# Moving the split of the unit of weights three ahead in front of the step of the side work

## The chip, the cores and the metric

The kernel runs on one core of a Trainium2 chip. The metric is the device time of one execution, in microseconds (us). TensorE (PE in the profile) multiplies matrices, ScalarE (ACT), VectorE (DVE) and GpSimd (POOL) do the elementwise work, and SyncE (SP) issues nearly all transfers from HBM.

## The reference

Two transformer blocks follow each other on one sequence of 256 tokens with 1024 features, all in fp32. What is computed, cut to the calls:

```python
# first block
proj = rmsnorm(x, norm_mix_pre) @ w_in            # split into ten parts
ya = gla_mixer(...) @ w_branch_a                  # chunked gated linear attention
yb = pool_mixer(...) @ w_branch_b                 # trailing means
yc = moba_mixer(...) @ w_branch_c                 # softmax attention with a bias
mixed = gs0 * ya + gs1 * yb + gs2 * yc            # sigmoid gates
x = x + rmsnorm(mixed @ w_out, norm_mix_post)
h = rmsnorm(x, norm_ffn_pre)
x = x + rmsnorm((silu(h @ w_gate) * (h @ w_up)) @ w_down, norm_ffn_post)
# second block
x = x + 0.5 * swiglu(rmsnorm(x, ffn1_norm), ...)
x = x + hybrid_mixer(rmsnorm(x, mix_norm), ...)   # compressed, selected, windowed and forgetting attention
x = x + memory_cross_attention(rmsnorm(x, mem_q_norm), rmsnorm(mem, mem_kv_norm), ...)
x = x + 0.5 * swiglu(rmsnorm(x, ffn2_norm), ...)
return rmsnorm(x, final_norm)
```

## The kernel before

All large products run on one pattern. The weights are cut into 360 units of 128 x 1024 fp32 numbers at most (512 KB). SyncE fetches unit u into one of four buffers `raw` (line 2263). ScalarE writes its upper part `whi` (function `split` of `scalar`, line 1262), VectorE the lower part `wlo` (`split` of `vector`, line 1596). Both go into one of four slots (`NSPL = 4`). Then TensorE multiplies the unit in three passes: upper by upper, lower by upper, upper by lower (lines 829 to 831 or 837 to 840), 12 or 24 matmuls in some 2.7 us. ScalarE may write slot u only when unit u-4 has been multiplied (`used`), and SyncE may fetch unit u+4 when `wlo` of unit u is there.

Every engine walks through the same plan, the generator `order`, and issues its own share in that order:

- "unit": the products of one unit, on TensorE alone.
- "split": the split of one unit, on ScalarE, VectorE and SyncE. `split_to(u)` issues all splits up to unit u that are still missing.
- "step", from `tick`: one step of each task that is under way, on all engines. Tasks are the work beside the products: `gla`, `moba`, `fox`, `cmp`, the ends of the feed-forward layers (`turn`), and the norms.
- "end": the copying out of a finished product's banks.

In `product` and `woven` the order for a unit u is: `split_to(u + 2)` (`AHEAD = 2`), unit u, `tick()`, and behind the last unit of a product its end. So ScalarE and VectorE meet: step of u, end, split of u+3, step of u+1, split of u+4. When TensorE begins unit u, the splits up to u+2 stand ahead of it in the queues.

The steps that the prediction speaks of:

- `rest(i)`, one for each of seven norms. Its first step (`norm_root`) turns sums of squares into 1/root: VectorE line 1632, GpSimd `power` (2180, 2183), VectorE `rstd` (1620 to 1626). Two to seven steps later `across` writes `diag` on VectorE (line 1642), TensorE spreads it (line 872), and VectorE copies it to `rT` (line 1645). TensorE waits in its queue for `diag`.
- `gla`: ScalarE takes exp and ln (lines 1350, 1352) in step 2, VectorE subtracts (line 1765) and sums in step 3, forms levels in steps 4 and 5, ScalarE takes exp (line 1357) in steps 6 and 7, VectorE scales into `lKQ` (line 1806) in step 7, and TensorE multiplies that (line 905) from step 9 on. In step 22 two chains of `rstd` and two products (lines 1836, 1839) give `m_gr`, which TensorE transposes (line 858) in step 24. The steps of `gla` start behind unit 9, so step 2 stands behind unit 11.
- `pool`: GpSimd builds trailing sums (lines 2215 to 2230). GpSimd reaches it as soon as its part of `gla` is done.
- `rel`: SyncE moves a table of 2 MB from HBM to HBM in a strided form (`wide`) and reads it back (line 2257).
- The gates `mixed` (lines 1699, 1701), the ends of the branch products.

The two lines of `product` around which the change is made:

```python
yield "unit", name, j, u
...
yield from tick()
```

Of the kernel before, what the change touches and what calls it, by code (L numbers as in the profile page):

```python
# [23 lines left out]
AHEAD = 2  # L24
# [281 lines left out]
def order(chunks, n_units):  # L306
# [4 lines left out]
    def split_to(u):  # L311
        while split[0] <= min(u, n_units - 1):
            yield "split", None, 0, split[0]
            split[0] += 1

    def tick():
        for name in list(left):
            yield "step", name, 0, 0
            left[name] -= 1
            if not left[name]:  # L320
                del left[name]
                for n in THEN.get(name, ()):
                    spawn(n)
# [6 lines left out]
    def spawn(name):  # L330
        left[name] = STEPS[name]
# [4 lines left out]
    def product(name, mid={}, end_first=False, ahead=0, open_end=False):  # L336
        for j, u in enumerate(chunks[name]):
            yield from split_to(u + AHEAD)
            if j in mid:
                yield from mid[j]()  # L340
            yield "unit", name, j, u
            if end_first and u == chunks[name][-1]:
                yield "end", name, 0, 0
            yield from tick()
            if u == chunks[name][-1]:
                yield from split_to(u + ahead)
        if not end_first and not open_end:
            yield "end", name, 0, 0
# [7 lines left out]
    def ffn(i, mid={}):  # L356
        for c in range(11):
            yield from product(f"f{i}gu{c}", mid if c == 0 else {})
            spawn(f"turn{i}_{c}")

    def woven(halves, mid={}, then={}, ahead=0):

        n = len(chunks[halves[0]]) // 2
        for i, (name, j) in enumerate((name, j) for first in (0, n) for name in halves for j in range(first, first + n)):
            u = chunks[name][j]
            yield from split_to(u + AHEAD)
            if i in mid:
                yield from mid[i]()
            yield "unit", name, j, u
            yield from tick()  # L370
            if u == chunks[halves[1]][-1]:
                yield from split_to(u + ahead)
            if j == 2 * n - 1:
                yield "end", name, 0, 0
                if name in then:
                    spawn(then[name])
# [10 lines left out]
    for n in range(3):  # L387
        yield from do(f"quarter0_{n}")
        yield from split_to(n)
    yield from product("qk", {0: more_x, 1: x_squared}, open_end=True)  # L390
    yield from product("g1")
    yield "end", "qk", 0, 0
    yield from product("gv")
# [13 lines left out]
    for n in range(2):  # L407
        for i in range(3):
            yield from product(f"br{i}{n}")
        spawn(("mixed_first", "mixed_second")[n])  # L410
    yield from woven(("wo0", "wo1"), ahead=AHEAD + 1)
    yield from drain()
    yield from do("sum0")
# [43 lines left out]
    yield from drain()  # L457
    spawn("y_second")
    yield from woven(("mo0", "mo1"), then={"mo0": "first5"})
    yield from drain()  # L460
    yield from woven(("cq0", "cq1"), {1: at_once("second5")}, {"cq0": "mem0", "cq1": "mem1"})
    for h in (2, 3):
        yield from product(f"cq{h}", end_first=True)
# [1991 lines left out]
```

## Time and profile before

| | us |
|---|---|
| median of 3 executions | 1131.37 |
| lowest and highest | 1130.27, 1132.52 |
| the profiled execution's own time | 1130.39 |
| its span, first to last instruction | 1128.6 |
| TensorE busy in the span | 1103.1 |
| VectorE busy | 720.9 |
| ScalarE busy | 557.2 |
| GpSimd busy | 22.8 |

The mean granted TensorE clock is 0.996. One reads this page from TensorE's row: it is busy for 98% of the span, so what a change in the order can give or take is the time in which TensorE stands still, and who ends each such wait. The busy shares of the other engines tell little; in the attention stages their queues are full, in the feed-forward layers they are half empty.

### The profile page before, as it was taken

What the parts mean: (1) busy time and instruction counts of PE and PEld (TensorE: products, weight loads), DVE (VectorE), ACT (ScalarE), POOL (GpSimd) and SP (SyncE); (2) the same over time, 40 slices, a digit from 0 to 9 for tenths busy, and PEclk for the clock granted to TensorE, in tenths of its full rate; (3) what the DMA queues carried; (4) which work ended last, traced back from release to release, by engine and by line L of the source; (5) the groups of instructions that cost most, each with busy time, mean ns of one, the idle gap of its engine ahead of it and who ended that gap; (6) DMA issues with size and microseconds to landing.
All of it is one profiled execution on the core that took longest, in us unless ns stands there. A gap on an engine that the chain in (4) does not pass through costs nothing.

```text
span 1128.6 us, 18330 instructions
## 1 busy us (share of the span) xinstructions
PE 1103.1 (98%) x7610; PEld 993.1 (88%) x7610; DVE 720.9 (64%) x1085; ACT 557.2 (49%) x838; POOL 22.8 (2%) x43
## 2 busy tenths in 40 slices
PE   8999999999999999999999999999999999999996
PEld 8888878789999988899998899898788989999985
DVE  5686765867666655566666554767666657666652
ACT  5643575546444544544354445446645545444442
POOL 0000400000000000000000000000000000000000
PEclk9999999999999999999999999999999999999998
DMA  8645545565666665676776568224365435565661
GB/s 285 198 150 168 167 163 187 212 202 165 193 198 191 220 204 159 205 260 199 252 253 212 186 205 280 94 96 138 125 240 168 138 125 187 187 206 188 202 205 59
DMA packets 63374, 210.79 MB, mean 187 GB/s; under 512 B 7387, under 2 KB 14731, under 8 KB 62396
## 3 DMA queue, kind: packets, MB, share of 16 engines
q1 hardware_dynamic: 63004, 209.53, 56.2%
q8 instruction: 60, 0.98, 0.4%
q14 instruction: 22, 0.18, 0.0%
q10 hardware_dynamic: 288, 0.10, 0.0%
HBM read 206.44 MB, written 5.26 MB: 188 GB/s over the span
## 4 chain that ended last, share of the span: by engine, by line
PE 83%; DVE 8%; ACT 3%; DMA 3%; issue 1%; POOL 0%; SPq 0%; DVEq 0%; POOLq 0%; ACTq 0%
PE ps L837 13%; PE ps L839 13%; PE ps L840 13%; PE ps L829 12%; PE ps L831 12%; PE ps L830 12%; DMA raw<-in_wflat 2%; DVE wlo_b L1596 1%; DVE wlo L1596 1%; PE ps L994 1%; PE ps L858 1%; PE ps L980 1%; DMA x<-in_x 1%; ACT whi_b L1262 1%; PE ps L905 1%
## 5 line engine op out<-in xcount | busy, mean ns | idle before, releaser
L837 PE MATMUL ps<-hT_hi,whi_b 128*128 128x256 f32 x1392 | 388.4, 279 | 3.8 <-DVE wlo_b L1596 3.8
L839 PE MATMUL ps<-hT_hi,wlo_b 128*128 128x256 f32 x1392 | 385.4, 277 | 0.0
L840 PE MATMUL ps<-hT_lo,whi_b 128*128 128x256 f32 x1392 | 385.3, 277 | 0.0
L1596 DVE TENSOR_TENSOR wlo_b<-raw,whi_b 128x1024 fp32r<-128x1024 f32 (+1 forms) x184 | 219.6, 1212 | 113.6 <-ACT whi_b L1262 113.4
L1596 DVE TENSOR_TENSOR wlo<-raw,whi 128x1024 fp32r<-128x1024 f32 x176 | 212.5, 1224 | 116.1 <-ACT whi L1262 115.4
L837 PEld LDWEIGHTS ps<-hT_hi,whi_b 128*128 128x128 f32 x1392 | 262.1, 188 | 7.9 <-issue 5.2
L839 PEld LDWEIGHTS ps<-hT_hi,wlo_b 128*128 128x128 f32 x1392 | 262.2, 188 | 0.3
L840 PEld LDWEIGHTS ps<-hT_lo,whi_b 128*128 128x128 f32 x1392 | 262.1, 188 | 0.0
L1262 ACT ACTIVATE whi<-raw 128x1024 fp32r<-128x1024 f32 x176 | 182.3, 1056 | 115.7 <-PE ps L831 94.2
L1262 ACT ACTIVATE whi_b<-raw 128x1024 fp32r<-128x1024 f32 (+1 forms) x184 | 184.6, 1042 | 35.3 <-PE ps L831 15.2
L829 PE MATMUL ps<-whi,hT_hi 128*128 128x512 f32 (+1 forms) x256 | 101.5, 396 | 3.1 <-DVE m_gqk L1660 1.6
L829 PE MATMUL ps<-whi,f_hid_hi 128*128 128x512 f32 x264 | 102.8, 389 | 0.0
L830 PE MATMUL ps<-wlo,f_hid_hi 128*128 128x512 f32 x264 | 102.7, 389 | 0.0
L831 PE MATMUL ps<-whi,f_hid_lo 128*128 128x512 f32 x264 | 102.7, 389 | 0.0
L831 PE MATMUL ps<-whi,hT_lo 128*128 128x512 f32 (+1 forms) x256 | 98.2, 384 | 0.0
L830 PE MATMUL ps<-wlo,hT_hi 128*128 128x512 f32 (+1 forms) x256 | 98.2, 383 | 0.0
L1332 ACT ACTIVATE f_sg<-f_sg 128x512 f32<-128x512 f32 x33 | 20.9, 633 | 124.0 <-DVE f_sg L1739 124.0
L829 PEld LDWEIGHTS ps<-whi,hT_hi 128*128 128x128 f32 x256 | 48.1, 188 | 16.3 <-issue 3.9
L831 PEld LDWEIGHTS ps<-whi,f_hid_lo 128*128 128x128 f32 x264 | 49.6, 188 | 10.3
L830 PEld LDWEIGHTS ps<-wlo,f_hid_hi 128*128 128x128 f32 x264 | 49.6, 188 | 10.2
L829 PEld LDWEIGHTS ps<-whi,f_hid_hi 128*128 128x128 f32 x264 | 49.6, 188 | 10.2
L831 PEld LDWEIGHTS ps<-whi,hT_lo 128*128 128x128 f32 x256 | 48.1, 188 | 9.7
(323 smaller groups left out, 1262.8 us busy)
## 6 DMA issues: line engine op xcount, KB each, us to landing
raw<-in_wflat SPq DMA_DIRECT2D x358, 512.0 KB, 3.9
wide<-scratch SPq DMA_DIRECT2D x1, 2048.0 KB, 10.7
m_w<-in_cmp_k_w SPq DMA_DIRECT2D x4, 512.0 KB, 6.1
m_w<-in_cmp_v_w SPq DMA_DIRECT2D x4, 512.0 KB, 6.4
m_alibi<-in_c_alibi SPq DMA_DIRECT2D x1, 1536.0 KB, 7.4
m_xT<-in_xT SPq DMA_DIRECT2D x4, 256.0 KB, 5.8
x<-in_x SPq DMA_DIRECT2D x2, 512.0 KB, 8.0
m_memT<-in_memT SPq DMA_DIRECT2D x1, 1024.0 KB, 5.8
```

Source lines behind the costliest of these rows:

```text
L829: e.matmul(o, xh, hi[:, k, :], start=first and k == 0, stop=False)
L830: e.matmul(o, xh, lo[:, k, :], start=False, stop=False)
L831: r = e.matmul(o, xl, hi[:, k, :], start=False, stop=last and k == kt - 1)
L837: e.matmul(o, hi[:, k, c], xs.h(k0 + k), start=first and k == 0 and f % 2 == 0, stop=False, skip_group_check=True)
L839: e.matmul(o, lo[:, k, c], xs.h(k0 + k), start=False, stop=False, skip_group_check=True)
L840: r = e.matmul(o, hi[:, k, c], xs.l(k0 + k), start=False, stop=last and k == kt - 1, skip_group_check=True)
L858: r = e.transpose(s[:, 256 * i + 128 * t:256 * i + 128 * t + 128], src(t)[:, 128 * (f + i):128 * (f + i) + 128], ident)
L905: r = e.matmul(ss[par][:, 128 * i:128 * i + 128], kk, qq, start=True, stop=True)
L980: r = e.transpose(s[:, 128 * i:128 * i + 128], Ps[qb][:, h, 128 * k:128 * k + 128], ident)
L1262: e.activation(slot(whi, u)[:, 0:k * n], raw[u % NRAW][:, 0:k * n], ACT.Copy).then_inc(*w_hi.did(u))
L1332: e.activation(b, b, ACT.Silu).then_inc(*silu.did(i, c))
L1596: e.tensor_tensor(slot(wlo, u)[:, 0:k * n], r, h.bitcast(F32), ALU.subtract).then_inc(*w_lo.did(u))
```

## The change

Behind each unit u, and ahead of the step of the side work, a call of `split_to(u + 1 + AHEAD)` is put in, in both `product` and `woven`. On ScalarE, VectorE and SyncE the order becomes: split of u+3, step of u, end, split of u+4, step of u+1. The call at the head of the next unit then finds nothing to do. No instruction is added or removed. Only the places of the splits in the queues of ScalarE, VectorE and SyncE move, by one step and one end.

```diff
@@ -341,6 +341,7 @@
             yield "unit", name, j, u
             if end_first and u == chunks[name][-1]:
                 yield "end", name, 0, 0
+            yield from split_to(u + 1 + AHEAD)
             yield from tick()
             if u == chunks[name][-1]:
                 yield from split_to(u + ahead)
@@ -367,6 +368,7 @@
             if i in mid:
                 yield from mid[i]()
             yield "unit", name, j, u
+            yield from split_to(u + 1 + AHEAD)
             yield from tick()
             if u == chunks[halves[1]][-1]:
                 yield from split_to(u + ahead)
```

## Rows read from the trace of the kernel before

**Rows 1.** The page, part 1: busy us, share of the span, instructions.
```profile
PE 1103.1 (98%) x7610; PEld 993.1 (88%) x7610; DVE 720.9 (64%) x1085; ACT 557.2 (49%) x838; POOL 22.8 (2%) x43
```

**Rows 2.** Waits of PE: who waited for whom, us in total, times, longest.
```profile
PE ps L837 <- DVE wlo_b L1596: 3.8, 6, 0.9
...
PE ps L829 <- DVE wlo L1596: 1.4, 2, 0.9
PE ps L858 <- DVE m_mixed L1701: 1.6, 2, 0.8
```

**Rows 3.** Costliest groups: busy, mean ns of one, idle before, releaser.
```profile
L1596 DVE TENSOR_TENSOR wlo_b<-raw,whi_b 128x1024 fp32r<-128x1024 f32 (+1 forms) x184 | 219.6, 1212 | 113.6 <-ACT whi_b L1262 113.4
L1262 ACT ACTIVATE whi_b<-raw 128x1024 fp32r<-128x1024 f32 (+1 forms) x184 | 184.6, 1042 | 35.3 <-PE ps L831 15.2
```

**Rows 4.** Waits of ACT, in the columns of Rows 2.
```profile
ACT whi L1262 <- PE ps L831: 94.2, 63, 4.0
```

**Rows 5.** Timelines of DVE and PE, 22 to 24: start us, us, instruction [idle before].
```profile
22.27 0.48 DVE L1642 TENSOR_SCALAR diag<-cst,stat 128x128 f32<-128x128 f32 x2
...
23.30 0.60 PE L872 MATMUL ps<-diag,ones 128*128 128x128 f32 x4
```

**Rows 6.** Timelines of DVE and PE ahead of the first feed-forward layer, 262 to 274.
```profile
262.53 1.29 DVE L1660 SCALAR_TENSOR_TENSOR m_ckT<-ps,rT 128x512 f32<-128x512 f32 x2
...
271.15 0.48 DVE L1642 TENSOR_SCALAR diag<-cst,stat 128x128 f32<-128x128 f32 x2
...
273.06 0.61 PE L872 MATMUL ps<-diag,ones 128*128 128x128 f32 x4
```

**Rows 7.** Timeline of PE at the norm of the memory queries.
```profile
884.27 0.71 PE L872 MATMUL ps<-diag,ones 128*128 128x128 f32 x4 [0.53 <-DVE diag L1642]
```

**Rows 8.** Timeline of ACT in the gla stage, 42 to 45.
```profile
42.20 0.62 ACT L1350 ACTIVATE m_lab<-m_lab 128x512 f32<-128x512 f32 x1
42.84 1.28 ACT L1352 ACT_TABLE_LOAD   x1
...
44.68 1.04 ACT L1262 ACTIVATE whi_b<-raw 128x1024 fp32r<-128x1024 f32 x1
```

**Rows 9.** Timeline of DVE in the gla stage, 46 to 66.
```profile
46.90 0.68 DVE L1765 TENSOR_TENSOR m_lmn<-m_lmn,m_lab 128x512 f32<-128x512 f32 x1
...
62.34 1.23 DVE L1596 TENSOR_TENSOR wlo_b<-raw,whi_b 128x1024 fp32r<-128x1024 f32 x1 [1.79 <-ACT whi_b L1262]
63.48 2.83 DVE L1806 TENSOR_TENSOR m_lKQ<-m_gqk,m_lE 128x256 f32<-128x256 f32 x8
```

**Rows 10.** Timeline of PE in the gla stage, 60 to 69.
```profile
60.69 0.36 PE L837 MATMUL ps<-hT_hi,whi_b 128*128 128x256 f32 x1 [0.93 <-DVE wlo_b L1596]
...
66.60 1.16 PE L905 MATMUL ps<-m_lKQ 64*128 64x128 f32 x16
...
68.70 0.39 PE L837 MATMUL ps<-hT_hi,whi_b 128*128 128x256 f32 x1 [0.94 <-DVE wlo_b L1596]
```

**Rows 11.** Timeline of DVE at the end of the gla stage, 116 to 125.
```profile
116.98 1.95 DVE L1620 TENSOR_TENSOR sm<-sm 128x4 f32<-128x4 f32 x1
...
119.17 1.39 DVE L1624 TENSOR_SCALAR sm<-sm 128x4 f32<-128x4 f32 x1
...
122.17 2.90 DVE L1596 TENSOR_TENSOR wlo<-raw,whi 128x1024 fp32r<-128x1024 f32 x2
```

**Rows 12.** Timeline of POOL in the same stretch.
```profile
116.87 2.05 POOL L2218 TENSOR_TENSOR m_t<-m_pu 128x1084 f32<-128x1084 f32 x1
119.00 1.54 POOL L2220 TENSOR_TENSOR m_t<-m_t 128x807 f32<-128x807 f32 x1
```

**Rows 13.** Timeline of PE in the same stretch.
```profile
122.30 1.09 PE L858 MATMUL ps<-cst,m_gr 128*128 128x128 f32 x8
123.97 0.50 PE L829 MATMUL ps<-whi,hT_hi 128*128 128x512 f32 x1 [0.58 <-DVE wlo L1596]
```

**Rows 14.** Timeline of PE behind the transfer of the strided table.
```profile
567.25 0.35 PE L837 MATMUL ps<-hT_hi,whi_b 128*128 128x256 f32 x1 [0.53 <-DVE wlo_b L1596]
```

## The prediction, made before the changed kernel was run

> **What bounds the kernel now.** I read the page's busy line first: TensorE is busy for 1103.1 of 1128.6 us [rows 1]. So no order of the other queues can give back more than 25 us, and most of that is not to be had. Next the waits of TensorE: the waits for a lower half `wlo` of a unit sum up to 3.8 + 1.4 = 5.2 us in eight places [rows 2]. The timeline shows where: two lie in the first 18 us (0.6 each), where no split can come earlier, because the data has just landed. The other six are 0.93 and 0.94 in the gla stage [rows 10], 0.58 at its end [rows 13], 0.87 at the branch products, and 0.18 and 0.53 behind the strided table [rows 14]. That is 4.0 us, the most that earlier splits can give directly. The waits of ScalarE then tell how deep the splits run already: in 63 places ScalarE sits idle ahead of a split until TensorE has left the slot [rows 4], for 94.2 us. There the split already stands as early as four slots allow.
>
> **What the change does to a queue.** The order of splits and steps alternates as before, but each split stands one step further ahead. A split costs 1.04 us on ScalarE and 1.21 us on VectorE [rows 3], so its lower half is there 2.3 us after TensorE has left the slot. It matters what starts a step.
>
> A step that TensorE starts (an eviction at the end of unit u, the softmax behind scores) is not delayed. The split of u+3 waits for the end of unit u-1, is done 2.3 us later, and unit u ends some 2.7 us later. Where the queues are full, the split of u+4 simply takes the place that the split of u+3 had. I followed moba, fox, cmp, sel, win and the memory heads through the timeline and find every step in its old place: zero.
>
> A step that ScalarE, VectorE and GpSimd start among themselves, and that ran ahead of TensorE, now has one more split in front of it, and that split waits for TensorE. These steps are `rest`, parts of `gla`, and nothing else that I find. Their slack towards TensorE decides.
>
> **Norms.** `across` writes `diag`, and TensorE stands in its queue for it. At the start `diag` ends at 22.75 and TensorE takes it at 23.30, a slack of 0.55 [rows 5]. The split of unit 7 (1.2 us) now stands ahead of it, and the small split of unit 4 (0.3) ahead of the root but not of anything new: diag at 24.05, TensorE +0.8 us. Ahead of the first feed-forward layer `diag` ends at 271.63 and TensorE takes it at 273.06, slack 1.4 [rows 6]. Here the eviction of `m_ckT` (1.29) ran before in a gap in which VectorE waited for a split. It now stands behind that split, and one split more stands before `diag`: 1.29 + 1.2 - 1.4, with small overlaps, is +0.95 us. Before the third product of the memory keys, at 466, the same pattern repeats with the same slack: +0.9. At the norm of the memory queries TensorE waits already 0.53 [rows 7], so nothing absorbs the split: +1.15. The other three norms repeat the pattern with slacks of 2.5, 1.5 and 0.7; there the split waits for TensorE's slot and then takes 2.3 us on two engines, which brings `diag` to 0.3, 0.35 and 0.5 us behind TensorE. Sum of the seven: 0.8 + 0.95 + 0.9 + 1.15 + 0.3 + 0.35 + 0.5 = +4.95 us. Bounds: 0, if all is absorbed, and 7 x 1.2 = 8.4.
>
> **Gla, first chain.** Step 2 on ScalarE is exp at 42.20 and, with a table load of 1.28, ln until 44.77 [rows 8]. Both ran inside unit 10. Now the split of unit 14 precedes them, which waits for unit 10 to end at 43.44 and takes 1.05: exp at 44.55, ln until 47.1, +2.35 us. VectorE's `m_lmn` was at 46.90 [rows 9]. The split of unit 15, whose upper half comes behind ln, now stands before it: 49.35, +2.45. VectorE is full from there to 59.4, so the levels come 2.45 later, at 61.85. ScalarE's exp follows until 63.8 and its split of unit 19 until 64.8, VectorE's of 19 until 66.0, and `m_lKQ` (2.83) ends at 68.8 instead of 66.31. TensorE wants it for line 905, which began at 66.60 [rows 10] after a wait of 0.93 for `wlo` of unit 17. That wait goes, 0.5 for unit 18 comes, and TensorE arrives at 66.1 and waits 2.7 for `m_lKQ`. Then it does not wait for unit 19, where it waited 0.94. Unit 19 starts at 69.95 instead of 68.70: net +1.25 us. Bounds: -1.9 (both waits gone, nothing late) and +2.5.
>
> **Gla, end.** The split of unit 34 (1.2 us, its upper half at 116.2) now stands ahead of the first of two `rstd` chains, which ran from 114.85. The chain then begins at 117.45, inside GpSimd's long sums [rows 12]. In the trace two small instructions of the second chain, 0.16 us by nature, take 1.95 and 1.39 there, and end when a GpSimd instruction ends [rows 11, 12]. If the first chain meets these two stretches, it ends at 122.25, where the second did. The second, at least 2.2 us of work, ends at 124.45, or 125.5 if it is held twice again. TensorE is at line 858 at 122.30, with no slack at all [rows 13]. So line 858 comes 2.2 to 3.2 us later and the wait of 0.58 behind it goes: +1.6 to +2.6. I take +2.4, nearer to the upper end, since the rows show two holds per chain. Without any hold the second chain would end at 121.85 and the term would be -0.6.
>
> What the rows show here, two VectorE instructions held to the end of a GpSimd instruction [rows 11, 12], agrees with the Trainium skill, "SBUF — State Buffer", section "Who interferes with whom": VectorE and GpSimd share one pair of ports under an exclusive lock, and whoever starts first keeps it for the whole instruction. By that rule the moved split, which starts before GpSimd's first sum, would also hold GpSimd back by some 0.5 us, and the term would be +2.9 instead of +2.4.
>
> **Branch products.** At 224.78 TensorE waits 0.87 for `wlo` of unit 65. With the change this half is there four us earlier. But the gates `m_mixed` are made on a full VectorE queue whose order does not change, and TensorE waits for them at line 858 in two places, for 1.6 in all [rows 2]. It arrives 0.87 earlier at the second and waits 0.87 longer: zero.
>
> **Strided table.** The split of unit 186 waited for its data, which stood behind 2 MB. SyncE now passes that fetch before the table (the split of unit 182 moves ahead of the step that issues it), and TensorE's waits of 0.18 and 0.53 go [rows 14]: -0.7 us. The other transfers that SyncE is moved past (memory inputs at 193, the attention bias at 136, the weights at 665) keep their place, because the split ahead of them is itself done one step earlier.
>
> **Sum.** 4.95 + 1.25 + 2.4 + 0 - 0.7 = +7.9 us. The profiled execution took 1130.39 (span 1128.6, 1.8 around it), which gives 1138.3. The median of the runs is 1.0 above it: 1139.3. In the feed-forward layers, over half of the units, I expect no difference.
>
> **Rivals.**
> - *Earlier splits pay.* The chains that I delay have cover that I misjudge, for instance because ScalarE reaches them earlier. Then the 4.0 us of waits for `wlo` go, less the 0.87 that turn into a wait for gates: 3.1 to 4.0 us, 1127.4 to 1128.3. For it speaks that these waits are real; against it that line 858 at 122.30 and `diag` at 884.27 have no slack [rows 7, 13], so any delay there shows. It decides if the delayed steps come less than their slack late.
> - *The two cancel.* Only the steps without slack lose: 1.15 + 0.8 + some 2 for gla against 3.1 of gains. Net within 1.5 us: 1130 to 1133.
> - *A small loss.* VectorE's chain at the end of gla is not held by GpSimd (-0.6 instead of +2.4) and the norms lose half or all: 2.5 + 1.25 - 0.6 - 0.7 = +2.4, or +4.9: 1133.8 to 1136.3.
> - *The loss spreads.* Both gla terms at their upper bounds (2.5 and 2.6) and the norms at 7: 2.5 + 2.6 + 7 - 0.7 = +11.4, and TensorE's longer pauses might bring another stretch of a lower clock. About 1143 to 1146.
>
> **How the numbers follow.** Forecast (5 to 11 us slower) 0.53; small loss 0.14; spreads 0.08; cancel 0.15; splits pay 0.10. What can be told from no change is about 0.2%, 2.3 us. Faster 0.10, same 0.15, slower 0.75. The range for 8 in 10 reaches from the cancelling case to the upper bound: 1131.5 to 1144.5. It leaves out the gain and part of the cancelling case below, and the worst of the last case above. The forecast's own range is 1136 to 1142.
>
> **What would show it.** Right: TensorE's waits for `wlo` fall to about 1.7 us; new waits of TensorE for `diag` at seven places, 5 to 6 us in all; a wait of 2 to 3 us for `m_lKQ` before line 905 near 66; one of 2 to 3 us for `m_gr` before line 858 near 123; no wait at 563 and 567; the waits for gates at the branch products longer by 0.9. Wrong: if `diag` is ready before TensorE at 273 and 466, my account of the queue is off; if line 858 comes on time, GpSimd's holds were the error; if feed-forward stages change, something is at work that I do not see.

## The result

The changed kernel takes 1141.74 us in the median (1138.17 to 1142.94, four executions), the kernel before 1130.82 us beside it (1130.05 to 1132.52). The ratio is 1.0093, 95% interval 1.0080 to 1.0105: slower by 10.9 us. The forecast was 1139.3 us, its own range 1136 to 1142, and the range for 8 in 10 went from 1131.5 to 1144.5. The profiled execution took 1141.74 us, its span is 1139.6 us and its mean granted clock 0.991, where it was 0.996.

The page of the kernel after, part 1 (busy us, share of the span, instructions) and TensorE's granted clock in 40 slices. It answers to [rows 1]:

```profile
PE 1107.4 (97%) x7610; PEld 996.8 (87%) x7610; DVE 729.1 (64%) x1085; ACT 568.3 (50%) x838; POOL 22.0 (2%) x43
PEclk9989999999999999999999999999999999999998
```

The same instructions are there as before. TensorE's busy time rises by 4.3 us, though its work is the same: a part of the loss is matmuls at half clock. The rest is waits (kernel after: us in total, times, longest), to be laid beside [rows 2]:

```profile
PE ps L874 <- DVE diag L1644: 5.0, 5, 1.9
PE ps L860 <- DVE m_mixed L1703: 2.8, 2, 2.2
PE ps L907 <- DVE m_lKQ L1808: 2.8, 1, 2.8
...
PE ps L839 <- DVE wlo_b L1598: 1.6, 3, 0.8
...
PE ps L860 <- DVE m_gr L1841: 0.2, 1, 0.2
```

In the code of the kernel after, each line of the engines has a number higher by 2 than before (872 is 874). In the experiments the shift is a few lines more; the tiles tell which instruction it is. (Waits of TensorE for `diag` stand in the trace at all seven norms, 5.3 us in all; the list leaves out two of 0.14 and 0.15 us.) The waits for `wlo` fell from 5.2 to 1.6 us, as forecast. In their place TensorE waits for `diag`, `m_lKQ` and `m_mixed`, and every one of these waits ends with VectorE.

Where the time goes is best read from the units. I took the start of each unit's first matmul in both traces and subtracted; each step of this difference is a place where time is lost or won. Everywhere else a unit follows the one before it at the same distance as in the kernel before, 2.72 us in the feed-forward layers. The last column is what of a step goes with a stretch at half clock: the step, less what the same place costs in a trace whose clock stays up there (norms_off, below).

| place (unit, us in the trace before) | forecast | after | of it at half clock |
|---|---|---|---|
| norm 0 (5, at 26) | +0.8 | +1.45 | |
| right behind it (6) | 0 | +1.52 | +1.5 |
| start of `gla` (17 to 20, at 61 to 73) | +1.25 | +3.99 | +2.95 |
| end of `gla` (34, at 124) | +2.4 | -0.70 | |
| branch products (60 to 67) | 0 | +1.4 | +1.6 |
| the norm at 238, of the memory (69) | +0.3 | +0.41 | |
| norm 1 (81) | +0.95 | +1.08 | |
| norm 2 (151) | +0.9 | +1.04 | |
| strided table (186 to 188) | -0.7 | -1.29 | |
| norm 3 (225) | +0.35 | +0.41 | |
| units 238 to 240 | 0 | -0.08 | -1.6 |
| norm 5 (281) | +1.15 | +1.32 | |
| norm 6 (298) | +0.5 | +0.58 | |
| sum | +7.9 | +11.1 | +4.5 |

TensorE's granted clock is a row of its own. Busy time and clock of TensorE in stretches, of the kernel after:

```profile
25.00:31.00 6.00, 4.37 (x14) 0.72 0.66 208
...
71.50:78.50 7.00, 6.69 (x39) 0.52 0.42 137
230.00:235.00 5.00, 2.79 (x14) 1.00 0.56 190
235.00:239.00 4.00, 4.00 (x16) 0.57 0.46 155
...
705.00:720.00 15.00, 15.00 (x125) 1.00 0.67 242
```

and of the kernel before, the same places:

```profile
25.00:31.00 6.00, 5.47 (x24) 1.00 0.56 190
...
71.50:78.50 7.00, 7.00 (x73) 1.00 0.68 226
...
235.00:239.00 4.00, 4.00 (x21) 1.00 0.84 281
716.00:719.40 3.40, 3.40 (x17) 0.50 0.00 0
```

The columns are the stretch, its length, TensorE busy (instructions), granted clock, share of the DMA engines, GB/s. The kernel after has three stretches at 1.2 instead of 2.4 GHz: from 27.0 us on for 3.4, from 71.4 for 6.8 and from 235.2 for 3.4. At each TensorE was standing still or just had (1.2 and then 1.6 us before 27.15, 2.8 before 71.81, 2.2 before 234.85). The kernel before has one such stretch, at 716 us, and after has none there. Every execution that was profiled has one more over its last microseconds; it is left out from here on.

### The profile page after: what moved, and what is told of

Same layout as the page of the kernel before. It is cut to its first block, busy times and chain, and to the rows that moved or that the text cites. A ratio compares the mean times of both kernels' runs of the same rounds, so it can differ in the third digit from the quotient of the medians.

```text
span 1139.6 us, 18349 instructions
## 1 busy us (share of the span) xinstructions
PE 1107.4 (97%) x7610; PEld 996.8 (87%) x7610; DVE 729.1 (64%) x1085; ACT 568.3 (50%) x838; POOL 22.0 (2%) x43
## 4 chain that ended last, share of the span: by engine, by line
PE 81%; DVE 9%; ACT 5%; DMA 2%; issue 2%; POOL 1%; SPq 0%; DVEq 0%; POOLq 0%; ACTq 0%
PE ps L839 13%; PE ps L841 12%; PE ps L842 12%; PE ps L831 12%; PE ps L832 12%; PE ps L833 12%; DVE wlo L1598 2%; DVE wlo_b L1598 1%; DMA raw<-in_wflat 1%; ACT junk L1289 1%; PE ps L996 1%; PE ps L860 1%; ACT whi L1264 1%; PE ps L907 1%; PE ps L982 1%
## 5 line engine op out<-in xcount | busy, mean ns | idle before, releaser
L1598 DVE TENSOR_TENSOR wlo_b<-raw,whi_b 128x1024 fp32r<-128x1024 f32 (+1 forms) x184 | 222.4, 1214 | 135.6 <-ACT whi_b L1264 132.3
L1598 DVE TENSOR_TENSOR wlo<-raw,whi 128x1024 fp32r<-128x1024 f32 x176 | 215.4, 1227 | 146.1 <-ACT whi L1264 144.8
L1264 ACT ACTIVATE whi<-raw 128x1024 fp32r<-128x1024 f32 x176 | 185.8, 1058 | 172.5 <-PE ps L833 144.6
L1264 ACT ACTIVATE whi_b<-raw 128x1024 fp32r<-128x1024 f32 (+1 forms) x184 | 191.4, 1047 | 93.7 <-PE ps L842 54.6
L1334 ACT ACTIVATE f_sg<-f_sg 128x512 f32<-128x512 f32 x33 | 20.9, 632 | 79.8 <-DVE f_sg L1741 79.8
```

The costliest lines, as they stand in the source:

```text
L1264: e.activation(slot(whi, u)[:, 0:k * n], raw[u % NRAW][:, 0:k * n], ACT.Copy).then_inc(*w_hi.did(u))
L1334: e.activation(b, b, ACT.Silu).then_inc(*silu.did(i, c))
L1598: e.tensor_tensor(slot(wlo, u)[:, 0:k * n], r, h.bitcast(F32), ALU.subtract).then_inc(*w_lo.did(u))
```

## The experiments

Where an edit stands in `product` and `woven` alike, one of the two places is shown. All times are medians; "before" is the kernel before, run beside each group: 1130.07 us for the first four, 1129.68 for the second four, 1129.88 for the next three, 1129.73 for the last.

| kernel | us | ratio to before (95%) |
|---|---|---|
| start_off | 1137.40 | 1.0057 (1.0041 to 1.0073) |
| norms_off | 1131.36 | 1.0009 (1.0000 to 1.0019) |
| gla_end_only | 1130.05 | 0.9999 (0.9989 to 1.0008) |
| quiet_only | 1133.95 | 1.0030 (1.0018 to 1.0041) |
| fill | 1138.30 | 1.0071 (1.0057 to 1.0085) |
| act_early | 1122.75 | 0.9936 (0.9922 to 0.9949) |
| ends_only | 1141.09 | 1.0097 (1.0084 to 1.0111) |
| picked | 1128.32 | 0.9985 (0.9976 to 0.9994) |
| pause | 1161.79 | 1.0286 (1.0265 to 1.0307) |
| dve_late | 1122.70 | 0.9937 (0.9922 to 0.9952) |
| inner_only | 1132.99 | 1.0029 (1.0016 to 1.0042) |
| six_lower | 1129.11 | 0.9995 (0.9986 to 1.0004) |

**start_off.** The early split only from unit 37 on:

```diff
-            yield from split_to(u + 1 + AHEAD)
+            if u >= 37:
+                yield from split_to(u + 1 + AHEAD)
```

> The changed kernel with the early split left out behind units 0 to 36, so that the order of the work up to the end of `gla` is that of the kernel before. Theory (the chains between ScalarE, VectorE and GpSimd at the first norm and at the start of `gla` pay, with the two stretches at half clock behind them): the +6.5 us that unit 34 was late in the trace after go, 1141.7 - 6.5 = 1135.2 us, and no half-clock stretch near 27 or 72 us. Rival (every split that is done a step earlier costs the same, wherever it stands): 34 of the 235 moved splits are put back, 34/235 of 10.9 us = 1.6 us, so 1140.1 us.

1137.4 us (1134.8 to 1138.5): 4.3 us of the expected 6.5 come back. Up to unit 60 the units stand where they stand in the trace before. Behind them the steps at the norms and at the table are there again to 0.1 us: 1.07 at unit 81, 1.05 at 151, 0.41 at 225, 1.31 at 281, 0.58 at 298. The profiled execution (1138.5 us) gives back 3.2 us, and what it lacks is the clock: it is at half at 229, as in the kernel after, and also at 707 and 891 us, which cost 1.5 us at units 235 and 236 and 1.6 us at unit 282, where the kernel after had none. So these steps belong to their places and add up, and the rival, an equal price for each split, is out. Half-clock stretches do not keep their places.

**norms_off.** The early split left out while a norm's chain is under way:

```diff
+            if not any(n[:4] == "rest" or n[:6] == "second" for n in left):
                 yield from split_to(u + 1 + AHEAD)
```

> The changed kernel with the early split left out while the rest of a norm's work (`rest*`, `second*`) is under way, 25 splits in all. Theory (a split that waits for TensorE stands ahead of the norm's short ScalarE steps, so TensorE waits for `diag`): the seven steps at the norms go, 1.45 + 0.41 + 1.08 + 1.04 + 0.41 + 1.32 + 0.58 = 6.3 us, and with the first of them the half-clock stretch at 27 us, 1.5 us: 1133.9 us; 1135.4 us if that stretch has nothing to do with the wait. Waits of TensorE for `diag` fall from 5.0 us to about 0.5. Rival (every early split costs the same): 25/235 of 10.9 us = 1.2 us, 1140.5 us.

1131.36 us: with a small part of the moved splits put back, 10.4 of the 10.9 us are gone. (The expectation says 25 of 235. Counted from the order that the two kernels produce, 278 splits change their place in the queues against the kernel before, and this edit puts 20 of them back.) The steps at the norms, but for the memory's (unit 69, +0.41, whose chain this condition does not name), are at zero. It is 2.5 us better than expected. In the profiled execution, whose time is the median, two waits of TensorE that are still there (2.73 us for `m_lKQ` at 68.74 and 2.21 us for `m_mixed` at 228.78) are not followed by half clock, which is worth 4.5 us; a stretch at 703 us takes 1.6 back. So only some 6 us of the 10.4 are the norms themselves, and the rest is clock. This gives the price of these places without the clock: the start of `gla` +1.04 us (-1.09, +0.36, +1.77), the branch products +0.14 (-1.16, +1.30 at units 65 and 66; -0.17 over units 60 to 67, where the kernel after has +1.43).

**gla_end_only.**

```diff
+            if 29 <= u <= 36:
                 yield from split_to(u + 1 + AHEAD)
```

> The kernel before with the early split behind units 29 to 33 alone (splits 32 to 36), the stretch of the end of `gla`. By the trace after: TensorE's wait at line 858 falls from 0.6 to 0.2 us and the following units start 0.7 us earlier, 1130.8 - 0.7 = 1130.1 us. By the prediction on record (the split stands in front of the squares, and GpSimd's two instructions hold a longer chain): +2.4 us, 1133.2 us.

The edit reaches three units further than the expectation says. By the order it moves six splits, 32 to 36 and 39.

1130.05 us. In the trace unit 34 starts 0.80 us earlier than before, 0.70 of it at this place, and the span is 0.7 us shorter (1127.9). The medians do not show it; their ratio is known to 0.1%. What the run excludes is the +2.4 of the prediction at this place.

**quiet_only.**

```diff
+            if all(n[:4] == "turn" for n in left):
                 yield from split_to(u + 1 + AHEAD)
```

> The kernel before with the early split only where nothing is under way beside the products but the turns of the gated units (93 splits, all in the three feed-forward parts). Theory (an early split costs only where a chain of steps stands behind it, and gives back the wait for the split at the strided table of f1): -1.3 us, 1129.5 us. Rival (each early split costs the same): 93/235 of 10.9 us = +4.3 us, 1135.1 us.

1133.95 us, 3.9 slower than before. The theory missed by 4.5 us; the rival's number is 1.2 us off, but the loss is not spread as it wants: 1.2 us at units 189 and 190 and 3.4 us in three equal steps at 271, 279 and 295, where this kernel moves no split by a step. The condition also holds where nothing at all is under way, and there, with no step between, the split moves in front of the product's `end`. By the order these are 48 splits beside the 93 that the expectation counts. Timelines of VectorE and TensorE, quiet_only:

```profile
848.90 2.36 DVE L1600 TENSOR_TENSOR wlo<-raw,whi 128x1024 fp32r<-128x1024 f32 x2
851.18 0.68 DVE L1703 TENSOR_TENSOR m_ytmp<-ps,m_gg 128x512 f32<-128x512 f32 x1
...
854.07 1.06 PE L862 MATMUL ps<-cst,m_y 128*128 128x128 f32 x8 [1.36 <-DVE m_y L1705]
```

Two lower halves in a row stand in front of the evictions, which come 1.14 us later against TensorE than before, where the second stood behind them. TensorE's wait for `m_y` is 1.36 us (0.21 in the kernel before). The same happens ahead of units 279 and 295. In the kernel after it does not, since there the first of the two lower halves was moved as well and has been done before the evictions are due. So whether an early split costs or is free depends on what was moved around it.

**fill.** TensorE works while it waits, in the kernel after:

```diff
+                        if pr == 0 and pair == 0:
+                            fill(ss[0], 14)
                         q.wait_ge(*gla_v.at("scaled", pr))
...
+            def fill(s, n):
+                for _ in range(n):
+                    e.matmul(s[:, 0:128], ones[:, :], ones[:, :], start=True, stop=True)
```

> The changed kernel, with 14 matmuls of `ones` by `ones` on TensorE in front of its wait for `m_lKQ` (2.77 us in the trace after) and 11 in front of its wait for the second half of `m_mixed` (2.21 us); they write a bank that the work behind them writes anew. Theory (the half-clock stretch is released by TensorE's idle stretch): no half-clock stretch near 71 and 235 us; units 19 and 20 behind `gla`'s first levels are 3.1 us less late and units 66 and 67 1.2 us less, 1141.7 - 4.3 = 1137.4 us. Rival (the clock falls in these places for another reason, or anywhere): the stretches are still there, 1141.7 us. With the four traces so far, in which the same 2.2 us wait was followed by full clock once and by half clock twice, the chance of the theory is no more than even.

1138.3 us, 3.4 less than the kernel after. Timeline of TensorE, and two stretches with the clock, fill:

```profile
66.79 3.18 PE L855 MATMUL ps<-ones 128*128 128x128 f32 x27
69.90 1.16 PE L918 MATMUL ps<-m_lKQ 64*128 64x128 f32 x16
```

```profile
71.20:78.00 6.80, 6.80 (x66) 1.00 0.63 181
231.00:235.00 4.00, 4.00 (x21) 1.00 0.45 142
```

The matmuls of `m_lKQ` are no earlier than they were, but what follows runs at full clock: units 19 and 20 win 2.6 us, units 66 and 67 win 1.5 us. For these two places the execution agrees with the theory, but it does not settle it. The stretch at 27 us, where nothing was changed, is gone too (1.5 us), the clock is at half at 707, 721 and 892 us instead, and in norms_off the same two waits, with nothing in them, were followed by full clock as well.

**act_early.** Each engine gets its own order; only ScalarE's has the early split, the others keep that of the kernel before.

```diff
-            for what, name, j, u in plan:
+            for what, name, j, u in plan_early if early else plan:
...
         def scalar(q):
-            run(q, split=split, end=ended,
+            run(q, early=True, split=split, end=ended,
```

> The kernel before in the order of every engine but ScalarE: only ScalarE's order has the early split, the lower halves on VectorE stand where they stood. In the trace after, VectorE's `diag` at the norms starts right behind a lower half of a split (281.81 and 894.32 us), one more than before. Theory V (the norms' cost is one lower half of 1.22 us more in front of `diag` on VectorE): the seven steps at the norms, 6.3 us, are not there; what is left is the start of `gla`, where ScalarE's exponential stands behind a split that waits for TensorE, at most 2 us: 1130 to 1132 us. Theory S (the cost is ScalarE's wait for TensorE inside the split, in front of ScalarE's steps of the chains): the steps stay, 1137 to 1141 us.

1122.75 us (1122.66 to 1122.93): faster than before by 0.64%, and 19.0 us faster than the kernel after. The steps at the norms are gone, as theory V says. Neither theory expected a gain: the time lies 7 us below the lower end of V. This settles the engine. ScalarE's chain steps do run late: at the start of `gla` (timelines of ScalarE and VectorE, act_early)

```profile
43.71 1.06 ACT L1267 ACTIVATE whi_b<-raw 128x1024 fp32r<-128x1024 f32 x1 [2.17 <-PE ps L836]
...
46.60 0.63 ACT L1357 ACTIVATE m_lab<-m_lab 128x512 f32<-128x512 f32 x1
...
47.27 0.69 DVE L1770 TENSOR_TENSOR m_lmn<-m_lmn,m_lab 128x512 f32<-128x512 f32 x1 [1.24 <-ACT m_lab L1357]
```

ln ends at 47.23, 2.46 us later than before [rows 8], which is the prediction's 2.35. But `m_lmn` starts at 47.27, only 0.37 later than before [rows 9]. In the kernel after the same instruction waits for a lower half in front of it:

```profile
51.20 1.23 DVE L1598 TENSOR_TENSOR wlo_b<-raw,whi_b 128x1024 fp32r<-128x1024 f32 x1 [2.19 <-ACT whi_b L1264]
52.34 0.68 DVE L1767 TENSOR_TENSOR m_lmn<-m_lmn,m_lab 128x512 f32<-128x512 f32 x1
```

That is the kernel after; `m_lmn` runs 5.4 us later than in the kernel before, and 2.3 us later than TensorE's own lateness of 3.1 us explains. ScalarE's share of the delay is absorbed, VectorE's is not.

It also shows what the early upper half is worth where VectorE is in a softmax. VectorE in the kernel before, and in act_early:

```profile
155.45 1.23 DVE L1596 TENSOR_TENSOR wlo<-raw,whi 128x1024 fp32r<-128x1024 f32 x1 [2.93 <-ACT whi L1262]
156.59 0.42 DVE L1888 CUSTOM_DVE_ANT_0 m_Pb<-ps,m_alibi 128x256 f32<-128x256 f32 x1
```

```profile
151.59 1.22 DVE L1601 TENSOR_TENSOR wlo<-raw,whi 128x1024 fp32r<-128x1024 f32 x1
153.35 0.42 DVE L1893 CUSTOM_DVE_ANT_0 m_Pb<-ps,m_alibi 128x256 f32<-128x256 f32 x1 [0.55 <-PE ps L1034]
```

Before, VectorE stood 2.93 us in front of a lower half whose upper half came behind ScalarE's exponentials, and the scores stood behind it. Now it goes through at once, and TensorE's waits of 1.19 us for `m_P` at 161 and of 1.66 us for `m_PcT` at 816 are gone. In the starts of the units the gain is 1.2 us at unit 19, 1.4 at 45, 0.6 at 60, 1.2 at 186 and 187, 1.7 at 260 and 0.8 each at 279 and 295: 7.7 in all.

**ends_only.** In the kernel before, the split behind the last unit of a product goes between the steps and the `end`:

```diff
             yield from tick()
             if u == chunks[name][-1]:
-                yield from split_to(u + ahead)
+                yield from split_to(u + max(1 + AHEAD, ahead))
...
             if j == 2 * n - 1:
+                yield from split_to(u + 1 + AHEAD)
                 yield "end", name, 0, 0
```

> The kernel before with one split moved per product alone: the one behind the last unit goes in front of the product's `end` (its evictions), but stays behind the steps. By the kernel with early splits in the quiet stretches, whose waits for `m_y` and `x` grew by 1.14, 1.14 and 1.13 us at units 271, 279 and 295: a lower half of 1.22 us now stands in front of evictions that TensorE's transposes wait for, at these three places and at the branch products (wait for `m_mixed`) and the sums at 263 and 457 us: +3.4 us for three places, up to +7 us for six: 1133.5 to 1137 us. Rival (at these places a lower half is hidden, and the growth there came from something else): 1130 us.

1141.09 us: the price is there and larger than my range of 1133.5 to 1137. The three places give 1.14 each again. What I had left out are evictions for which other work waits: `m_gqk` at 26 us (TensorE waits 2.57 instead of 1.63), `m_mixed` (2.68 instead of 0.82), and `cm_cqT` at 899.6 us (2.11 instead of none); behind each of these three the clock was at half, at 26.2, 231.0 and 900.1 us. This kernel moves 83 splits in front of ends and loses as much as the kernel after, which moves the same 83 and 195 more; the prices do not add up from kernel to kernel.

**picked.**

```diff
+            if 29 <= u <= 33 or 154 <= u <= 201:
                 yield from split_to(u + 1 + AHEAD)
```

> The kernel before with the early split only behind units 29 to 33 (the end of `gla`) and 154 to 201 (the feed-forward part of the strided table), where the trace after was 0.7 and 1.3 us ahead and no norm and no branch eviction stands behind it. If the steps add up: units from 190 on start 2.0 us earlier; some of it is given back at the waits for `m_R` and `m_PT0f` near 725 us: 1128.5 to 1129.5 us against the 1130.1 us of the kernel before. Rival (the early split gives nothing that lasts): 1130.1 us.

1128.32 us, ratio 0.9985 (0.9976 to 0.9994): 1.4 us faster than before and a little below the range expected. Unit 187 starts 2.4 us earlier, as the steps add up (1.9 from the two places, the rest smaller ones).

**pause.** In the kernel before, TensorE waits ahead of four units for a split that is further on:

```diff
                 q.wait_ge(*w_lo.at(u))
+                if (name, j) in (("f0gu6", 1), ("f2gu4", 1)):
+                    q.wait_ge(*w_hi.at(u + 3))
+                if (name, j) in (("f0gu9", 1), ("f2gu7", 1)):
+                    q.wait_ge(*w_lo.at(u + 3))
```

> The kernel before with four pauses of TensorE put into quiet feed-forward stretches, where nothing waits: two at which TensorE waits for the upper half of the split three units on (near 331 and 985 us, some 1.3 us each) and two at which it waits for that split's lower half (near 363 and 1018 us, some 2.5 us each). If the clock falls to half behind every pause of over 2 us: two stretches at half clock, right behind 363 and 1018 us, 1130.4 + 2 x 1.3 + 2 x 2.5 + 2 x 1.7 = 1141.4 us. If the clock falls without regard to pauses: 1130.4 + 7.6 = 1138.0 us. By the seven traces so far (a wait of 2.1 us and more was followed by half clock in 6 of 10 cases) I expect one of the two stretches and 1138 to 1141 us.

1161.8 us; I had mis-sized the pauses. They are 4.4 and 5.7 us, since the awaited split stands behind another split and a step. Timeline and stretches of TensorE, pause:

```profile
334.84 0.36 PE L841 MATMUL ps<-hT_hi,whi_b 128*128 128x256 f32 x1 [4.44 <-ACT whi_b L1266]
375.08 0.55 PE L841 MATMUL ps<-hT_hi,whi_b 128*128 128x256 f32 x1 [5.70 <-DVE wlo_b L1600]
```

```profile
325.00:330.00 5.00, 5.00 (x46) 1.00 0.66 211
...
335.00:339.00 4.00, 4.00 (x22) 0.57 0.62 227
...
373.00:380.00 7.00, 4.92 (x23) 0.51 0.45 153
1001.00:1008.00 7.00, 4.97 (x23) 0.51 0.66 212
1042.00:1049.00 7.00, 5.07 (x24) 0.51 0.47 149
```

At each of the four, where nothing else was changed, the clock is at half; at three of them it fell while TensorE still stood. The pauses put the units 20.9 us back and the half clock 8.8 us more, 1.7 to 2.4 us each. That TensorE's standing still brings the half clock about is shown for pauses of this length: the fall comes at all four in the profiled execution and at none of these places in the other thirteen traces, and all four executions of this kernel have a lower mean clock (0.983 to 0.987) than any other. Shorter waits are followed by it at times: over the profiled executions of all these kernels in seven of nine cases after waits of 2.1 to 2.9 us (my count of six in ten ahead of this run was off; it was six in eight), in two of four after waits of 1.9 us, and in one of 27 after waits of 1.5 to 1.8 us, the one at 27 us with 1.2 us of standing still shortly ahead of it. And seven of the fourteen profiled executions, that of the kernel before among them, have a stretch between 702 and 725 us, where no such wait stands ahead. What sets those I have not found.

**dve_late.** The kernel after with VectorE's order alone undone (as act_early, with SyncE early too).

> The changed kernel with one engine's order undone: VectorE's is that of the kernel before, ScalarE's and SyncE's have the early split. ScalarE's alone gave 1122.8 us. Theory (all of the loss is the place of the lower halves in VectorE's queue; SyncE's order carries nothing, since its fetch waits for the lower half anyway): 1122.5 to 1123.5 us, no wait of TensorE for `diag` but the one of before near 878 us, and the gain at the strided table (units 186 and 187, 1.2 us) stands as it does with ScalarE's order alone. Rival (SyncE's order takes part, fetches move in front of the other transfers and these come late): 1125 to 1131 us.

1122.7 us, as expected. No unit differs from act_early by a lasting step. SyncE's order carries nothing, and the whole loss of 19.0 us between this kernel and the kernel after comes from where the lower halves stand in VectorE's queue, the clock that falls in its wake included. In the profiled executions the units are 19.1 us apart at the end: 6.1 of it are the seven norms, 6.1 the three stretches at half clock, 2.2 the start of `gla` without the clock, and 5.1 the gains at units 45, 60 to 67, 260, 279 and 295 that ScalarE's order alone brings and the kernel after does not have; the end of `gla` gives 0.8 back, and smaller steps make up the rest.

**inner_only.** The kernel after without the early split behind the last unit of each product:

```diff
+            if u != chunks[name][-1]:
                 yield from split_to(u + 1 + AHEAD)
```

> The changed kernel without the early split behind the last unit of each product, so that no split moves in front of an `end`. Theory (two costs on VectorE's queue: a lower half in front of the norms' and gla's chains, and one in front of evictions): the chains' part stays, the wait for `m_mixed` at the branch products falls from 2.2 to some 1.9 us and the half-clock stretch behind it may go: 1141.7 - 0.5 to 2 = 1139.7 to 1141.2 us. Rival (the evictions are most of the loss, as the 11 us of the kernel with the splits in front of the ends alone suggest): 1131 to 1134 us.

1132.99 us, 8.7 less than the kernel after and 6.7 below the range that I expected. The rival's number is met, but not by its reason. The norms' steps are gone at all places but the memory's (+0.41), and the wait for `m_mixed` is 0.79. I had overlooked that the last step of a norm's chain, the one that writes `diag`, falls on the last unit of a product at each of the other six norms: units 4, 80, 150, 224, 280 and 297. So among the 86 splits that this kernel puts back are the six that stand in front of `diag` and that norms_off puts back too. It loses elsewhere: TensorE waits 2.88 us for `m_PcT` at 817 (1.66 in the kernel before), with half clock behind it.

**six_lower.** act_early, and on VectorE six lower halves in front of the norms' last step:

```diff
+    def norm_due():
+        return any(n[:4] == "rest" or n[:6] == "second" for n in left if left[n] == 1)
...
+            if early == 1 or early == 2 and norm_due():
                 yield from split_to(u + 1 + AHEAD)
```

> The kernel with ScalarE's order alone early (1122.8 us), and on VectorE six lower halves moved: those of units 7, 83, 153, 227, 283 and 300, which now stand in front of the step that writes `diag` (the last step of a norm's chain, which falls on the last unit of a product each time) instead of behind it and behind the product's end. Theory (one lower half of 1.22 us in front of `diag`, less the slack it had): the six steps of the trace after come back, 1.45 + 1.08 + 1.04 + 0.41 + 1.32 + 0.58 = 5.9 us, 1128.6 us, with waits of TensorE for `diag` of about 1.2, 0.8, 0.8, 0, 1.9 and 0.3 us, and 1130.3 us if the clock falls once behind them. Rival (the split pays in the chain only where both halves and the steps before `diag` are late too): at most 1 us, 1122.8 to 1123.8 us.

1129.11 us in the median (1126.90 to 1132.11), 6.4 more than act_early. Its profiled execution took 1126.9, 4.0 more than act_early's, and all of that is at the six units: 0.68, 0.68, 0.41, 0.41, 1.13 and 0.59. Their sum is 3.9, and the 5.9 that I had expected is half as much again. The rest of the median goes with a lower clock in the other eleven executions (0.993 to 0.996 against 0.997), which are 1.2 to 5.2 us longer than the profiled one. Waits of TensorE, first six_lower, then act_early:

```profile
PE ps L879 <- DVE diag L1649: 3.1, 4, 1.9
```

```profile
PE ps L877 <- DVE diag L1647: 0.8, 1, 0.8
```

Moving six instructions of 1.2 us by one place costs 4 us in the profiled execution, 6.4 in the median, and brings a wait of 1.9 us.

## Why the prediction was right, and where it was not

**The bound and the waits for `wlo`.** Right: 5.2 us of waits fell to 1.6 (forecast 1.7), and the feed-forward layers, over half of the units, show no difference.

**Norms.** Right in place, sign and pattern; the term was +4.95 and measured 6.3, with the largest miss at norm 0 (+0.8 against +1.45). That miss is largely this execution's: the data of unit 5 lands later, so its upper half starts at 19.51 us where it started at 17.89 in fill, and `diag` at 24.27 instead of 23.56. In fill, whose order is the same there, the step is +0.84. Timeline of VectorE and TensorE at norm 1 in the kernel after, beside [rows 6]:

```profile
278.33 0.16 DVE L1628 TENSOR_TENSOR stat<-stat,sm 128x2 f32<-128x2 f32 x1
278.40 3.49 DVE L1598 TENSOR_TENSOR wlo_b<-raw,whi_b 128x1024 fp32r<-128x1024 f32 x3
281.81 0.47 DVE L1644 TENSOR_SCALAR diag<-cst,stat 128x128 f32<-128x128 f32 x2
...
282.34 0.71 PE L874 MATMUL ps<-diag,ones 128*128 128x128 f32 x4 [0.82 <-DVE diag L1644]
```

`diag` could start at 278.5, when `stat` is there. It starts when the third lower half is through. At norm 5, which had no slack [rows 7], TensorE's wait rose from 0.53 to 1.93 us, but 0.17 of that is a gain of unit 280 ahead of it, so that units 280 and 281 together are 1.15 us late, the forecast:

```profile
892.05 2.35 DVE L1598 TENSOR_TENSOR wlo_b<-raw,whi_b 128x1024 fp32r<-128x1024 f32 x2
894.32 0.48 DVE L1644 TENSOR_SCALAR diag<-cst,stat 128x128 f32<-128x128 f32 x2
...
894.85 0.60 PE L874 MATMUL ps<-diag,ones 128*128 128x128 f32 x3 [1.93 <-DVE diag L1644]
```

The Trainium skill, "PSUM — Partial Sum Buffer", section "Engine vs sequencer instructions", says that ScalarE's and VectorE's queues are strictly first in, first out. These rows agree: a `diag` of 0.48 us whose operands are there stands 3.3 us behind lower halves at norm 1. Where the prediction spoke of ScalarE, VectorE and GpSimd together, act_early shows that the place in VectorE's queue is what counts.

**Gla, first chain.** The sum was right: +1.25 forecast, +1.04 measured where the clock stays up (norms_off), with the wait of 2.7 us for `m_lKQ` as forecast (2.77). In the kernel after 2.95 us of half clock come on top, which the prediction named only in the rival that the loss spreads. The prediction's chain is the one in the trace: ln is late, the upper half of unit 15 comes behind it, and its lower half stands in front of `m_lmn`, which is 2.3 us late for +2.45 forecast. What it did not say is that the last link decides: with ln as late and the lower half behind `m_lmn` (act_early), `m_lmn` loses 0.37 us.

**Gla, end.** Wrong: +2.4 forecast, -0.70 measured, and TensorE's wait at line 860 is 0.20 us, not 2 to 3. The step that failed is the first sentence of that part: it took the upper half of unit 34 as done at 116.2, as before. But it had run there only because the squares (line 1374) stood in front of it. Timelines of ScalarE and VectorE in the kernel before:

```profile
114.85 0.28 ACT L1374 ACTIVATE m_lE<-ps 128x128 f32<-128x128 f32 x1
...
115.10 1.08 ACT L1262 ACTIVATE whi<-raw 128x1024 fp32r<-128x1024 f32 x1
...
114.85 0.17 DVE L1620 TENSOR_TENSOR sm<-sm 128x4 f32<-128x4 f32 x1 [3.78 <-POOL sm L2183]
```

Timelines of ScalarE, VectorE and GpSimd, kernel after, in a trace that is 7.1 us late here:

```profile
118.63 1.06 ACT L1264 ACTIVATE whi<-raw 128x1024 fp32r<-128x1024 f32 x1 [1.66 <-PE ps L833]
119.60 0.26 ACT L1376 ACTIVATE m_lE<-ps 128x128 f32<-128x128 f32 x1
...
119.72 1.23 DVE L1598 TENSOR_TENSOR wlo<-raw,whi 128x1024 fp32r<-128x1024 f32 x1 [1.49 <-ACT whi L1264]
122.14 0.16 DVE L1622 TENSOR_TENSOR sm<-sm 128x4 f32<-128x4 f32 x1 [1.19 <-POOL sm L2185]
...
124.27 1.96 DVE L1622 TENSOR_TENSOR sm<-sm 128x4 f32<-128x4 f32 x1
...
124.04 2.16 POOL L2220 TENSOR_TENSOR m_t<-m_pu 128x1084 f32<-128x1084 f32 x1
```

The moved split runs in ScalarE's gap while TensorE still works on the values that are to be squared, its lower half is done 1.2 us before the `rstd` chain, and that chain starts at 122.14 - 7.14 = 115.0, where it was to 0.15 us. GpSimd's long sums meet the second chain as they did, and VectorE's 0.16 us instruction is again held for 1.96 us to the end of GpSimd's (126.20). This is one more row that agrees with the Trainium skill, "SBUF — State Buffer", section "Who interferes with whom", on which the prediction drew for the lock; the first chain was never late enough to meet it. The prediction had named a line 858 that comes on time as the sign that GpSimd's holds were the error. The sign came, but the hold is there; the error was the time of the moved split.

**Branch products.** Zero was forecast; without the clock it is +0.14 at units 65 and 66, with it +1.4 over units 60 to 67. The mechanism is the forecast one: TensorE comes earlier, by 1.16 us, and waits longer, 2.21 us where I had forecast 1.7. The reason given, that VectorE's order does not change there, is not right:

```profile
229.69 2.35 DVE L1598 TENSOR_TENSOR wlo<-raw,whi 128x1024 fp32r<-128x1024 f32 x2
231.97 0.68 DVE L1701 TENSOR_TENSOR m_mtmp<-ps,m_gates 128x512 f32<-128x512 f32 x1
...
234.85 1.58 PE L860 MATMUL ps<-cst,m_mixed 128*128 128x128 f32 x8 [2.21 <-DVE m_mixed L1703]
```

That is VectorE and TensorE of the kernel after. The lower half of unit 67 has moved in front of the end of `br21`, but that of unit 65 has moved away from there, so two stand in front of these evictions now as before, and the evictions end 0.14 us later against TensorE's own lateness. Where a second lower half comes in front of evictions and none leaves, as at the three places of quiet_only and ends_only, it costs 1.14 us. I had counted every `end` as "a step that TensorE starts", which the early split cannot delay; those two runs show that it can.

**Strided table.** -0.7 forecast, -1.29 measured. Both waits went, 0.18 and 0.53 [rows 14], and they gave back 0.35 and 0.85 us in the starts of the units. A wait costs more than its idle time in the profile: a unit that does not wait starts 0.17 us before the modelled end of the one before it (576.43 against 576.60 at unit 187), and unit 186, which waited in the kernel before, took 3.04 us there and 2.89 after. The prediction took the idle times as the price. SyncE does pass a fetch in front of the table in the kernel after, but that is not needed: act_early and ends_only, in which SyncE's order is that of before or nearly so, win the same 1.2 us at units 186 and 187. It is enough that lower halves are done earlier, since SyncE's fetch waits for them; in act_early the data of unit 186 is there 2.0 us into unit 184, before it was 3.4.

**The clock.** The missing term. Three half-clock stretches cost 6.1 us and one of before fell away (1.6). Norms (+1.35), `gla`'s end (-3.1), the table (-0.6), two small ones (-0.4) and the clock (+4.5, and +1.5 of waits at units 239 and 240 that the fast clock ahead of them uncovers) differ from the forecast by +3.2 together. Without the clock the measured steps sum to about 5.1 us, not 7.9. So the mechanism of the norms and of the start of `gla` was right, and that the total was hit closer than its terms was luck: a loss that the prediction left out of its sum stood in for one at `gla`'s end that did not come.

## What to carry to other kernels

When instructions are moved in a queue, take the time of the moved one anew: it starts when its own conditions are met, not where it stood in the old trace. A look-ahead that all engines share is a choice for each engine: here the half that waits for TensorE is worth starting a step earlier on ScalarE (-7 us), and the half on VectorE, whose queue holds short steps that TensorE waits for, is not (+19 us on top, 6 of them by the clock). VectorE's order alone, with ScalarE's as before, was not run. The fastest orders are those in which ScalarE runs ahead and VectorE does not.

## What the runs showed of the hardware

After TensorE has stood still, or while it still stands, its granted clock can fall to 1.2 GHz, for 3.4 or 6.8 us. Four waits of 4.4 and 5.7 us came with it four times, waits of 2.1 to 2.9 us seven times of nine, waits of 1.9 us twice of four, and waits of 1.5 to 1.8 us once of 27. The same wait of 2.2 us at the same place had full clock behind it once in three. A wait of 2.8 us filled with matmuls on `ones` was not followed by the fall, but neither was the same wait unfilled in norms_off. Where its price can be told apart, a stretch of 3.4 us costs 1.5 to 1.7 us and one of 6.8 us 2.3 to 3.0. The clock also falls between 702 and 725 us without such a wait, in seven of fourteen profiled executions. The four executions of the kernel after show how this moves a total: 1138.2 us at a mean clock of 0.994, 1141.7 twice at 0.991, 1142.9 at 0.990. In act_early, whose profiled execution has no such stretch, four executions lie within 0.3 us.
